# The recurrent stage of an RWKV-7 and attention trunk in steps of 512 tokens, its triangular inverse built on 32x32 blocks

## The reference, cut to what matters

```python
def step(state, inp):                 # for each of 1024 tokens, 12 heads, state 64 x 64
    r_t, w_t, k_t, v_t, kk_t, a_t = inp
    sa = einsum('bhvk,bhk->bhv', state, -kk_t)
    state = (state * w_t[:, :, None, :] + sa[..., None] * (kk_t * a_t)[:, :, None, :]
             + v_t[..., None] * k_t[:, :, None, :])
    return state, einsum('bhvk,bhk->bhv', state, r_t)
```

## Time and profile before

| | us |
|---|---|
| median of 3 runs (3391.11 to 3394.53) | 3391.24 |
| the profiled execution | 3393.09 |
| its span, first to last instruction | 3391.1 |

### The profile page before, as it was taken

How to read it: one execution, slowest core, us unless ns; L and a number is a source line. 1 busy time by engine, 2 the same in 40 slices (tenths; PEclk the granted TensorE clock), 3 DMA queues, 4 the chain that set the end, 5 groups by cost and what they waited for, 6 DMA issues and landing times. The chain is left out here.

```text
span 3391.1 us, 51704 instructions
## 1 busy us (share of the span) xinstructions
PE 3112.9 (92%) x22753; PEld 2494.3 (74%) x22753; DVE 1364.6 (40%) x1849; ACT 646.7 (19%) x1124; POOL 950.1 (28%) x670
## 2 busy tenths in 40 slices
PE   7999598888868999999999998979989999999998
PEld 6887376676756788888888776656657788888887
DVE  6333255554434342222222564736662531313232
ACT  4111332223213210000000213114441300100010
POOL 4342243332321333323332322210002323333321
PEclk9999698888878999999999998989999999999999
DMA  5331200000002111111111232231103111111111
GB/s 195 95 114 66 62 21 15 21 21 9 3 26 94 44 45 49 50 44 56 38 57 43 91 90 63 68 143 76 76 20 100 44 44 56 44 56 39 56 41 66
DMA packets 259494, 198.14 MB, mean 58 GB/s; under 512 B 32262, under 2 KB 244348, under 8 KB 257992
## 3 DMA queue, kind: packets, MB, share of 16 engines
q1 hardware_dynamic: 258520, 194.08, 18.5%
q10 hardware_dynamic: 272, 0.73, 0.1%
q0 software_dynamic: 480, 0.03, 0.0%
HBM read 155.44 MB, written 39.37 MB: 57 GB/s over the span
## 5 line engine op out<-in xcount | busy, mean ns | idle before, releaser
L207 POOL CAST w_hi_b<-w_raw_b 128x1024 fp32r<-128x1024 f32 (+2 forms) x195 | 188.1, 965 | 1720.8 <-PE ps L232 1355.2
L232 PE MATMUL ps<-h_hi_f,w_hi_b 128*128 128x512 f32 x1664 | 516.8, 392 | 16.4 <-DVE h_lo_f L454 9.1
L232 PE MATMUL ps<-h_lo_f,w_hi_b 128*128 128x512 f32 x1664 | 514.8, 391 | 0.0
L232 PE MATMUL ps<-h_hi_f,w_lo_b 128*128 128x512 f32 x1664 | 514.4, 390 | 0.0
L209 POOL TENSOR_TENSOR w_lo_b<-w_raw_b,w_hi_b 128x1024 fp32r<-128x1024 f32 (+2 forms) x195 | 430.5, 2208 | 15.6
L232 PEld LDWEIGHTS ps<-h_hi_f,w_hi_b 128*128 128x128 f32 x1664 | 313.3, 189 | 85.1 <-issue 17.5
L232 PEld LDWEIGHTS ps<-h_lo_f,w_hi_b 128*128 128x128 f32 x1664 | 314.1, 189 | 65.6
L232 PEld LDWEIGHTS ps<-h_hi_f,w_lo_b 128*128 128x128 f32 x1664 | 313.8, 189 | 65.5
L1735 DVE TENSOR_TENSOR x_res<-x_res,ps 128x1024 f32<-128x1024 f32 x64 | 78.1, 1221 | 365.0 <-PE ps L232 365.0
L232 PE MATMUL ps<-act_hi,w_hi_b 128*128 128x512 f32 x704 | 217.3, 390 | 2.5 <-DVE act_lo L1730 2.5
L232 PE MATMUL ps<-act_lo,w_hi_b 128*128 128x512 f32 x704 | 216.8, 389 | 0.0
(11 more groups left out here) (295 smaller groups left out, 4799.4 us busy)
## 6 DMA issues: line engine op xcount, KB each, us to landing
w_raw_b<-in_w_gate_up SPq DMA_DIRECT2D x88, 512.0 KB, 3.9
w_raw_b<-in_w_down SPq DMA_DIRECT2D x32, 384.0 KB, 3.6
w_raw_a<-in_a_w_in SPq DMA_DIRECT2D x23, 512.0 KB, 4.6
u_dram<-evac_a SPq DMA_DIRECT2D x23, 512.0 KB, 3.0
w_raw_b<-in_w_down SPq DMA_DIRECT2D x32, 320.0 KB, 3.3
x_dram<-x_res SPq DMA_DIRECT2D x2, 4096.0 KB, 15.1
w_raw_b<-in_w_out SPq DMA_DIRECT2D x16, 512.0 KB, 7.0
x_res<-x_dram SPq DMA_DIRECT2D x2, 4096.0 KB, 13.6
```

Of the source, the lines that this page charges most:

```text
L207: self.nc.gpsimd.tensor_copy(self.whi[:, r, 0:tiles, :], raw).then_inc(self.w_hi, 1)
L232: mm = nc.tensor.matmul(bank[:, 2 * slot + j, 0:n], w[:, k, :], h[:, k, j * n:(j + 1) * n], start=(k == 0 and a == 0 and b == 0), stop=(k ...
```

## The change

A step now covers two tiles (512 tokens), so there are 12 steps, two a pair (j = 0 and 1). The inverse is built on the 32x32 blocks on the diagonal only: 8 slots of 32 columns on four groups of 32 partitions, with 4 levels instead of 5; the two second products write one bank, and one DVE instruction of 512 columns adds both. The block beside the diagonal ones is formed last (last_first, last_second, and full, which bars reads). blocks (ACT) and diagonal (DVE) bring the diagonal blocks into place, diagonals (ACT) brings the finished ones into full. In each of the 4 levels the state passes two chunks. turn and products of the two next tiles stand in levels 1 and 3, first_terms in 2 and 4. products issues kk and r as separate matmuls.

The states stay in a ring of 4 instead of one for each chunk, fade moves from DVE to ACT, the raw kk from DVE to ACT, gain and bias of the group norm from DVE to ACT. g is no longer kept: its product is made in group_norm after scale and read from PSUM. POOL makes seeds and all joins of a step at once (joins), after the side work. Side work is indexed by the level l inside side_work: prepare(p+1) in the steps with j = 0, group_norm(p-1) in those with j = 1. SP loads k, then r, then v, each behind waits of its own. lora and gate0 lie in the residual's tensor X, which is free in this stage.

The core of the diff, PE first:

```diff
-        STEPS = T // 256
+        STEPS = T // 512
...
+                    for i in range(8):
+                        for rows in quarters:
+                            mm = mmul(ps[rows, 1, i * B:(i + 1) * B], join[rows, l - 1, i, :], inv[rows, s % 2, 0, i, :], start=True, stop=True)
+                    mm.then_inc(u_done, 1)
...
+                def level_second(s, l):
+
+                    pe.wait_ge(u_copied, LEVELS * s + l)
+                    for i in range(8):
+                        for rows in quarters:
+                            mmul(ps[rows, 0, i * B:(i + 1) * B], inv[rows, s % 2, 1, i, :], um[rows, i, :], start=True, stop=True)
+                    for i in range(8):
+                        for rows in quarters:
+                            mm = mmul(ps[rows, 0, 256 + i * B:256 + (i + 1) * B], um[rows, i, :], inv[rows, s % 2, 1, i, :], start=True, stop=True)
+                    mm.then_inc(x_done, 1)
...
+                    def side_work(l):
+                        if j == 0 and p + 1 < PAIRS:
+                            prepare(p + 1, ("z", "a", "kk_sum", "kk_bc", "rk")[l - 1])
+                        if j == 1 and p >= 1 and l < LEVELS:
+                            group_norm(p - 1, ("mean", "sum", "bc", "g")[l - 1])
+
+                    if s < S:
+                        seeds_across(s)
+                    for l in range(1, LEVELS):
+                        first, second = 2 * l - 2, 2 * l - 1
+                        if recur and l > 1:
+                            outputs(*before[first - 1])
+                        if recur and l in (1, 2, 4):
+                            read_state(*before[first])
+                        if ahead and l == 1:
+                            turn(2 * s + 2)
                         if s < S:
...
+                            level_first(s, l)
+                        if ahead and l == 3:
+                            turn(2 * s + 3)
+                        if recur and l == 3:
+                            read_state(*before[first])
+                        if ahead and l == 2:
+                            first_terms(2 * s + 2)
+                        if ahead and l == 4:
+                            first_terms(2 * s + 3)
                         if s < S:
...
+                            level_second(s, l)
+                        if recur:
+                            write_state(*before[first])
+                        if s < S:
+                            side_work(l)
+                        if recur:
+                            outputs(*before[first])
+                            read_state(*before[second])
+                        if ahead and l in (1, 3):
+                            products(2 * s + 2 + l // 2)
+                        if recur:
+                            write_state(*before[second])
+                    if recur:
+                        outputs(*before[7])
                     if s < S:
+                        last_first(s)
+                        last_second(s)
                         bars(s)
-                for stage in ("mean", "sum", "bc"):
+                        side_work(LEVELS)
+                for stage in ("mean", "sum", "bc", "g"):
```

ACT, POOL and DVE in the same loop:

```diff
+                        if j == 0 and p + 1 < PAIRS and l <= 4:
+                            prepare(p + 1, ("kk", "z", "a", "exp")[l - 1])
+                        if j == 1 and p >= 1 and l in (2, 4):
+                            group_norm(p - 1, "square" if l == 2 else "affine")
...
+                        if ahead and l == 1:
+                            tok_out(2 * s + 2)
+                        if recur and l == 3:
+                            y_out(2 * s - 2)
                         if s < S:
...
+                            level_out(s, l)
+                        if ahead and l == 3:
+                            tok_out(2 * s + 3)
+                        if ahead and l == 2:
+                            first_out(2 * s + 2)
+                        if ahead and l == 4:
+                            first_out(2 * s + 3)
+                        if s < S:
+                            side_work(l)
+                        if recur:
+                            fade(*before[2 * l - 2])
...
+                    if j == 0 and p + 1 < PAIRS:
+                        rsqrt(kk_ms, small, kk_rn, p + 1)
+                        features(p + 1)
+                    if j == 1 and p >= 1:
+                        rsqrt(gn_ms, small_gn, gn_rn, p - 1)
+                    if s + 1 < S:
+                        joins(s + 1)
...
+                            for stage in ((), ("scan",), ("kk_ms", "k", "rk"), ("kk", "decay", "b"), ("bonus",))[l - 1]:
+                                prepare(p + 1, stage)
...
+                    for l in range(1, LEVELS):
+                        if recur:
+                            sa_in(*before[2 * l - 2])
                         if s < S:
...
+                            dve.wait_ge(x_done, LEVELS * s + l)
+                            both = inv[:, s % 2].rearrange("p b i c -> p (b i c)")
+                            tt(both, both, ps[:, 0, :], ALU.add).then_inc(x_added, 1)
+                        if recur:
+                            new_state(*before[2 * l - 2])
+                        if recur:
+                            sa_in(*before[2 * l - 1])
+                        if ahead and l in (1, 3):
+                            masked(2 * s + 2 + l // 2)
+                        if recur:
+                            new_state(*before[2 * l - 1])
+                        if ahead and l in (1, 3):
+                            diagonal(2 * s + 2 + l // 2)
+                        if s < S:
+                            side_work(l)
```

More of the change, by code:

```diff
@@ L973, in products @@
                                 out = halves[x if i == 0 else 1 - x]
-                                first, second = 2 * i + gg, 4 + 2 * gg + x
-                                both = ps[out, 4 + h, :].rearrange("p (a c) -> p a c", c=C)[:, first:second + 1:second - first, :]
-                                mm = mmul(both, ak[hs, b, 2 * q + gg, (0, 1, 3, 2)[2 * x + i], :], kr[hs, b, :, one], start=True, stop=True)
+                                rows = ak[hs, p % 2, 2 * (t % 4) + gg, (0, 1, 3, 2)[2 * x + i], :]
@@ new lines, in y_out, with diagonals @@
+                def y_out(t):
+                    act.wait_ge(y_done, t + 1)
+                    for h, hs in enumerate(halves):
+                        done = copy(y[hs, pair_of(t) % 2, (t % 4) * 256:(t % 4 + 1) * 256], ps[hs, 2 + h, 256:512])
+                    done.then_inc(y_copied, 1)
+                def diagonals(s):
+                    act.wait_ge(x_added, (LEVELS - 1) * (s + 1))
+                    nc.scalar.activation(full[:, :, 0:B], inv[:, s % 2, 1], ACT.Copy, scale=self.const("first"))
+                    nc.scalar.activation(full[:, :, B:C], inv[:, s % 2, 1], ACT.Copy, scale=self.const("second")).then_inc(diag_full, 1)
@@ L1187, in _ @@
+                    if s < S:
+                        diagonals(s)
+                    if recur:
+                        y_out(2 * s - 1)
+                    if s < S:
+                        level_out(s, LEVELS)
+                        bars_out(s)
+                for stage in ("square", "affine"):
+                    group_norm(PAIRS - 1, stage)
             @block.gpsimd
@@ new lines, in _, with side_work @@
+                    p, j = s // STEPS, s % STEPS
+                    before = parts(s - 1)
+                    ahead = s + 1 < S
+                    recur = s >= 1
+                    def side_work(l):
+                        if j == 0 and p + 1 < PAIRS:
+                            for stage in ((), ("scan",), ("kk_ms", "k", "rk"), ("kk", "decay", "b"), ("bonus",))[l - 1]:
+                                prepare(p + 1, stage)
+                        if j == 1 and p >= 1:
+                            for stage in (("centre",), ("ms",), ("scale",), (), ("out",))[l - 1]:
+                                group_norm(p - 1, stage)
```

593 lines of the change are left out of this document (297 added, 296 removed).

## The result

The changed kernel takes 3488.84 us (median of 4 runs, 3481.36 to 3510.73) against 3391.18 for the kernel before, measured with it: a ratio of 1.029, 95% interval 1.026 to 1.032. I had forecast 3435 us, slower, with a range of 3340 to 3500. Direction and range hold; the size doesn't: the loss is 98 us where the sum said 44. The profiled execution has a span of 3491.1 us and a mean granted clock of 0.913 (before: 3391.1 and 0.950).

A forecast was written before the change was run, and what follows sets the result against it. Bare steps were taken as bound by PE's stream and the inverse chain, others by queued side items. Full pairs +18, pair 0 +7, pair 5 +3, start +4, end +8 and +4 gave +44 us: 3435 us, range 3340 to 3500.

The forecast's parts named there:

- I take 30%: Recurrent loop: PE's clock is low for 30% of a pair, adding 11 us to 97.6; bounds 0% and 50%.
- 37 us a pair if always low: Price of the 1.2 GHz clock in the loop: about 10 a step for chain, products and turns, 17 a pair for side products.
- Record time: First and second products of a level: a 32x32 record on four tiles costs 12 ns, between 8 and 15.
- The rival at 27 ns a record: PE's queue delivers a record per 27 ns: level 2.9 us longer, loop 149, kernel 3584 us; chance 0.06.
- The 97.6 at the high level: A pair at the high clock: two bare steps of 39.5 us plus 18.6 of side work, 6.5 less than before.
- the level of 6.87 us: One bare level: first and second products, copy, addition, and two chunks' states one after the other sum to 6.87 us.
- the side items of 18.6 us a pair: Features and group norm showing beside the recurrence: 13.3 us in a pair's first step, 5.3 in the second, instead of 40.1.
- The exponentials: Level 4 of a pair's first step: DVE's k and rk wait for exp on ACT, delaying the state by 5.85 us.
- Neither product hidden: Bare recurrence grows 7.5 us: half the levels, each carrying two chunks one after the other, with neither hiding a product.
- b beside the features: DVE's b runs beside GpSimd's features; such an addition takes 3.12 us there, 1.23 alone; up to 4 us a pair.
- Faster: Rival: records at 8 ns (40 us) and low share of 10% (37 us) give 3358 us; chance 0.27.
- What would show it: Steps about 40 us, 50 with features; some 4 us wait for cum; 12 ns records; clock under 0.9; end 12 longer.

The follow-up runs named there:

- the fillers: Changed kernel with one to three extra identity products per gap, before a level's second product and around the state writes, result unread: 3489.7 us.
- the dense ones: Changed kernel with five rows of independent small products behind the stage's last product, into PSUM nobody reads; run once: 3542.3 us.
- the move: Changed kernel with the next pair's two exponentials on ScalarE behind level 3's first fade instead of in level 4's place: 3457.3 us.
- the new order: Changed kernel with first product, first write, outputs, second read, second product, second write on PE, VectorE's queue reordered too (masks behind the second state): 3438.3 us.

## Why the prediction was right and wrong, point by point

**Where the time went.** Against before: pairs 1 to 4 +50 (forecast +18), pair 0 +21 (+7), pair 5 +15 (+3), the end +16 (+12), the start +2 (+4), and outside the stage some 5 us less. The signs were right in every stretch of the stage; the six pairs carry the error, 58 us, and the end 4, less 7 at the start and outside.

**The clock is the term that was mis-sized.** The step that failed is "I take 30%". I priced the clock at 37 us a pair if always low; the fit gives 43, and the slots above 4.2 a level, close to 37/8 = 4.6. But I took a share of 30%, and it was 55%: 0.55 x 37 = 20.4 in place of 11, 9.4 a pair. The bound of 50% was too low as well. Pairs 0 and 5 show the same: I gave their clock 6 and 6.6 us, a share of less than a fifth, and they stood at 59% and 75%. Why I missed: I let the new loop have the share of the old one's worst pair, though the same paragraph said that PE now waits for a quarter and more. PE's gaps of over 0.25 us in the loop rose from 65 (75 us) to 163 (147 us). The share is measured; that the time follows from it in full is by the price, and the fillers don't confirm it.

**Record time:** 12 ns taken, 8.9 found at the high level, the lower bound. 6.6 us a pair less. It hid about half of what clock and stops together added (9.4 and 4.5). By the Trainium skill, "TensorEngine Tiling (Array Packing)", Instruction Overhead, the repeat of a tile would have stayed; the trace disagrees: four tiles at 8.9 ns repeat every 36 ns.

**PE's queue.** The rival at 27 ns a record had the right number and the wrong reach: it holds for long rows (27 ns in the dense ones), while a level's 192 records run out of what is at hand now and then only. Its stops lasted 24.6 us, not 149. The forecast had no term between nothing and the full rival: 4.5 us a pair missing. With the stops all but gone the time fell by no more than the products left out were to bring, so they are no plain loss either. The Trainium skill, "TensorE: Matmul & The Clock Gate", "Wait — 56ns, not 53.3ns?", gives about 25 ns start to start at the least: bursts undercut it by nearly three times, long rows agree with it in size, though here the blocks of instructions set it.

**Together** for a pair: 108.6 - 6.6 + 4.5 + 9.4 = 115.9; measured 116.7. That it closes to 0.8 us is in part luck. The 97.6 at the high level less 6.6 is 91.0, but the fit's 90.5 has the stops in it and its 84.5 without them is 6.5 lower, while its price of the low level is 43 to 47 in place of 37. So the level of 6.87 us and the side items of 18.6 us a pair come out somewhat too long and the clock somewhat too cheap, and no run parts the two.

**The exponentials:** 5.85 us a pair, shown by the move (6.3). **Neither product hidden:** right in kind for the copy of um, whose wait of 11.6 us went with the new order; for tok_sv it is not shown. PE's waits for the state were longer, 42.5 us in the stage, and 27 of them went with that edit: the first new state stood in VectorE's queue behind the addition, which the sum had, the second in two levels of a step behind the masks, which the sum had only at what they cost before, within 2.7 us a tile. **b beside the features:** b's two operations took 1.22 us each, but for one of 3.07; the 4 us held ready for them were not needed.

**Rivals.** Faster: its first condition nearly came true (8.9 ns a record for 8), the second was far off (a low share of 55% in place of 10%), and both were needed. **What would show it:** bare steps of about 40 came at 46 to 47 and those with features at 62 to 64 (forecast 50), at a clock of 0.64 to 0.75. The granted clock came as said; the wait for cum was 5.5 us on average where some 4 were said, the end 16 us longer in place of 12.

## What to carry to other kernels

When a change makes an engine wait more, price the clock with the new idle share, not with the old kernel's, and give it the whole range up to always low. In a chain that crosses engines, look in every engine's queue for what stands ahead of the chain's own instructions: moving the exponentials (31.6 us), the masks (19.9) and, with them, the products and the addition (50.5) changed no work at all. Edits measured alone don't add up, and one that moves several queues doesn't show which of them gave the time. Count instructions as well as columns: small tiles in bursts are fast here (8.9 ns a record), but not in long rows (27 ns).

## What the runs showed of the hardware

- PE's instructions came in blocks of 256 records (16 KB), the next one 3.47 us after the last in dense rows. Stops of up to 2.2 us follow; the kernel before had none inside a run of products.
- Four 32x32 tiles side by side took 8.9 ns a record at the high clock and 13.3 at the low one: less than twice as long.
- VectorE's transpose of 32x32 blocks over 128x256 took 0.45 us; it replaced 64 records on PE.
- Of eleven stops of over 1.3 us that began at the high level ten had a lower granted clock in the 3 us behind them, but taking the stops away (22 to 6) didn't raise it: PE's gaps as a whole stayed (147 and 144 us), now waits for the chain.
